# A third buffer for raw weights in a two-layer hybrid encoder step, each unit one transfer with one signal

## The reference, cut to what matters

```
h  = rmsnorm(x, norm_mix)
z  = h @ w_in                     # one projection, 8208 columns: q, k, v | qg, kg, vg, rg | ag | ga, gb
oa = diff_attention(rope(q), rope(k), v, lam)      # 8 heads, two softmax maps a head, cached keys and values
og = gated_linear_attention(qg, kg, vg, decay(ag)) # 4 heads, in chunks of 64 tokens
ua = (rmsnorm(oa) * (1 - lam_init)) @ w_pa
ub = (rmsnorm(og) * silu(rg)) @ w_pb
x += (sigmoid(ga) * ua + sigmoid(gb) * ub) @ w_o
h  = rmsnorm(x, norm_ffn);  x += (silu(h @ w_f1) * (h @ w_f3)) @ w_f2      # inner width 2816
h  = rmsnorm(x, norm_ple);  x += sigmoid(h @ w_ple_gate) * (pe @ w_ple)
```

## Time and profile before

| | |
|---|---|
| time, median of 3 runs | 1424.36 us (1424.17 to 1426.08) |
| the profiled execution | 1431.38 us, its span 1429.6 us |
| PE busy | 1369.6 us, 96% of the span |
| DVE, ACT, POOL busy | 896.6, 620.7, 279.9 us |
| granted TensorE clock, mean | 0.983 of full speed |
| SP's transfers | 180.58 MB; 53.9% of 16 engines' span |
| the chain that ended last | PE 75%, DMA 12%, DVE 9% |

### The profile page before, as it was taken

How to read it: one execution, slowest core, us unless ns; L and a number is a source line. 1 busy time by engine, 2 the same in 40 slices (tenths; PEclk the granted TensorE clock), 3 DMA queues, 4 the chain that set the end, 5 groups by cost and what they waited for, 6 DMA issues and landing times.

```text
span 1429.6 us, 24105 instructions
## 1 busy us (share of the span) xinstructions
PE 1369.6 (96%) x9750; PEld 1326.4 (93%) x9750; DVE 896.6 (63%) x1455; ACT 620.7 (43%) x1043; POOL 279.9 (20%) x321
## 2 busy tenths in 40 slices
PE   6999989999999999999999999888999999999996
PEld 4999988899999999999989899888999999999995
DVE  3868647487666555555777585556775655555454
ACT  3454533546634333333445445334484343333332
POOL 1505031050023000022550231203200500001232
PEclk9999999999999999999999999999999999999998
DMA  7756598664444544444566559975534444454441
GB/s 165 133 119 139 106 107 112 130 139 135 145 139 150 156 147 148 154 146 161 125 117 110 121 134 113 117 99 117 133 125 161 140 151 153 148 157 134 152 150 44
DMA packets 194154, 190.62 MB, mean 133 GB/s; under 512 B 9046, under 2 KB 191132, under 8 KB 194044
## 3 DMA queue, kind: packets, MB, share of 16 engines
q1 hardware_dynamic: 188848, 180.58, 53.9%
q0 software_dynamic: 2688, 7.35, 1.4%
q10 hardware_dynamic: 2508, 1.16, 0.3%
HBM read 180.40 MB, written 8.65 MB: 132 GB/s over the span
## 4 chain that ended last, share of the span: by engine, by line
PE 75%; DMA 12%; DVE 9%; ACT 1%; issue 1%; POOL 0%; SPq 0%; DVEq 0%; POOLq 0%; ACTq 0%
PE big L1255 22%; PE big L1257 21%; PE big L1256 21%; DMA w_raw<-in_w_in 12%; DVE w_lo L849 3%; PE X L1541 1%; PE X L1434 1%; DVE ssq L1005 1%; DVE a_msk L996 1%; PE X L1297 1%; PE X L1466 1%; ACT w_hi L552 1%; PE X L1284 0%; DMA lrow<-in_lambda_k 0%; PE X L1384 0%
## 5 line engine op out<-in xcount | busy, mean ns | idle before, releaser
L1255 PE MATMUL big<-x_hi,w_hi 128*128 128x320 f32 x1856 | 590.7, 318 | 15.1 <-DVE z L939 12.8
L1256 PE MATMUL big<-x_lo,w_hi 128*128 128x320 f32 x1856 | 579.4, 312 | 0.0
L1257 PE MATMUL big<-x_hi,w_lo 128*128 128x320 f32 x1856 | 578.9, 312 | 0.0
L849 DVE TENSOR_TENSOR w_lo<-w_raw,w_hi 128x1024 fp32r<-128x1024 f32 (+1 forms) x328 | 418.6, 1279 | 165.4 <-ACT w_hi L552 163.4
L552 ACT CAST w_hi<-w_raw 128x1024 fp32r<-128x1024 f32 (+1 forms) x328 | 330.4, 1035 | 237.1 <-DMA w_raw<-in_w_in 135.3
L1255 PEld LDWEIGHTS big<-x_hi,w_hi 128*128 128x128 f32 x1856 | 354.1, 191 | 21.2 <-DVE z L939 14.3
L1256 PEld LDWEIGHTS big<-x_lo,w_hi 128*128 128x128 f32 x1856 | 354.1, 191 | 1.3
L1257 PEld LDWEIGHTS big<-x_hi,w_lo 128*128 128x128 f32 x1856 | 353.9, 191 | 0.0
L478 POOL TENSOR_TENSOR sqt<-xT 128x320 f32<-128x320 f32 x48 | 48.0, 999 | 604.8 <-DVE xT L1206 422.5
L1255 PE MATMUL big<-h_hi,w_hi 128*128 128x320 f32 x352 | 108.8, 309 | 0.0
L1257 PE MATMUL big<-h_hi,w_lo 128*128 128x320 f32 x352 | 108.6, 308 | 0.0
(11 more groups left out here) (250 smaller groups left out, 1932.0 us busy)
## 6 DMA issues: line engine op xcount, KB each, us to landing
w_raw<-in_w_in SPq DMA_DIRECT2D x128, 512.0 KB, 8.5
w_raw<-in_w_f SPq DMA_DIRECT2D x120, 512.0 KB, 4.4
w_raw<-in_w_pa SPq DMA_DIRECT2D x16, 512.0 KB, 4.5
w_raw<-in_w_pb SPq DMA_DIRECT2D x16, 512.0 KB, 3.9
w_raw<-in_w_o SPq DMA_DIRECT2D x16, 512.0 KB, 4.0
w_raw<-in_w_ple_gate SPq DMA_DIRECT2D x16, 512.0 KB, 4.7
w_raw<-in_w_f SPq DMA_DIRECT2D x16, 384.0 KB, 3.5
k_raw<-in_cache_k SPq DMA_DIRECT2D x8, 256.0 KB, 10.4
```

Source lines behind the costliest of these rows:

```text
L849: tt(w_lo[:, t % 4, 0:nk, :], w_raw[:, (t // 2) % 2, 0:nk, (t % 2) * P:(t % 2 + 1) * P], w_hi[:, t % 4, 0:nk, :].bitcast(F32), ALU.subtrac ...
L1255: mm(out, wh, xh[:, k0 + k, :], start=start and k == 0, stop=False)
L1256: mm(out, wh, xl[:, k0 + k, :], start=False, stop=False)
L1257: last = mm(out, wl, xh[:, k0 + k, :], start=False, stop=stop and k == nk - 1)
```

## The change

`w_raw` gets a third unit buffer. Where the slot of unit n was that of unit n - 2, it is that of unit n - 3, and SP waits for the splits of unit n - 3 instead of n - 2. A unit is issued as one transfer of 1 MB on one semaphore. Unit 0 of an iteration is still two transfers (qg and kg columns), now with a semaphore each: the `hi` of its first tile waits for the qg half alone (`qg_in`), that of its second tile for the buffer's own semaphore. To make room, `o_sq` no longer has a buffer but lies in the second part of `kcT`. The waits on raw weights are counted from the unit's number.

```diff
+RAW = 3
-    w_raw = sb("w_raw", [P, 2, KC, UW])
+    w_raw = sb("w_raw", [P, RAW, KC, UW])
-        o_sq = sb("o_sq", [P, T], where=where)
+    o_sq = kcT[:, :, :].rearrange("p a b -> p (a b)")[:, 2 * PAST - T:]
-    raw_in = [sem("raw_in0"), sem("raw_in1")]
+    raw_in = [sem(f"raw_in{i}") for i in range(RAW)]
+    qg_in = sem("qg_in")

+        def slot_free(tb, c):
+
+            n = tb // 2 + c
+            if n >= RAW:
+                sp.wait_ge(lo_ready, 2 * (n - RAW + 1) + CREDIT_TILE)
+            return n % RAW
+
         def unit(tb, c, src, row0, nrow, col0):
 
-            sp.wait_ge(lo_ready, tb + (2 * c + CREDIT_TILE - 2))
-            for r in range(0, nrow, nrow // 2):
-                sp.dma_start(w_raw[:, c % 2, r:r + nrow // 2, :],
-                             src[:, bass.ds(row0 + r, nrow // 2), bass.ds(col0, UW)]).then_inc(raw_in[c % 2], 16)
+            i = slot_free(tb, c)
+            sp.dma_start(w_raw[:, i, 0:nrow, :], src[:, bass.ds(row0, nrow), bass.ds(col0, UW)]).then_inc(raw_in[i], 16)
 
         def qk_unit(tb, l, j):
 
-            sp.wait_ge(lo_ready, tb + (CREDIT_TILE - 2))
+            i = slot_free(tb, 0)
             for half, col in enumerate((C_QG, C_KG)):
-                sp.dma_start(w_raw[:, 0, :, half * P:(half + 1) * P],
-                             w_in[:, bass.ds(l * KC, KC), bass.ds(j * P + col, P)]).then_inc(raw_in[0], 16)
+                sp.dma_start(w_raw[:, i, :, half * P:(half + 1) * P],
+                             w_in[:, bass.ds(l * KC, KC), bass.ds(j * P + col, P)]).then_inc(raw_in[i] if half else qg_in, 16)
...
-        def hi(tb, tb8, t, nk):
-
-            act.wait_ge(raw_in[(t // 2) % 2], tb8 + 32 * (t // 4 + 1))
+        def hi(tb, t, nk):
+
+            n = (tb + t) // 2
+            l, m = divmod(tb + t, TILES)
+            if m < MRG_0 and m % MIX_N == 0:
+                act.wait_ge(qg_in, 16 * (l * MIX_IT + m // MIX_N + 1))
+            else:
+                act.wait_ge(raw_in[n % RAW], 16 * (n // RAW + 1))
             act.wait_ge(tile_done, tb + (t + 1))
-            nc.scalar.copy(w_hi[:, t % 4, 0:nk, :], w_raw[:, (t // 2) % 2, 0:nk, (t % 2) * P:(t % 2 + 1) * P]).then_inc(hi_ready, 1)
+            nc.scalar.copy(w_hi[:, t % 4, 0:nk, :], w_raw[:, n % RAW, 0:nk, (t % 2) * P:(t % 2 + 1) * P]).then_inc(hi_ready, 1)
```

More of the change, by code:

```diff
@@ L547, in _ @@
     def _(act):
-        def hi(tb, tb8, t, nk):
-            act.wait_ge(raw_in[(t // 2) % 2], tb8 + 32 * (t // 4 + 1))
+        def hi(tb, t, nk):
[5 more added lines that the diff above has]
+                act.wait_ge(raw_in[n % RAW], 16 * (n // RAW + 1))
             act.wait_ge(tile_done, tb + (t + 1))
-            nc.scalar.copy(w_hi[:, t % 4, 0:nk, :], w_raw[:, (t // 2) % 2, 0:nk, (t % 2) * P:(t % 2 + 1) * P]).then_inc(hi_ready, 1)
+            nc.scalar.copy(w_hi[:, t % 4, 0:nk, :], w_raw[:, n % RAW, 0:nk, (t % 2) * P:(t % 2 + 1) * P]).then_inc(hi_ready, 1)
         def base(l, j, per, first):
-            return act.snap(l * TILES + j * per + first), act.snap(l * (8 * TILES) + j * (8 * per) + 8 * first)
+            return l * TILES + j * per + first
         def tables(which):
@@ L611, in _ @@
             if l == 0:
-                first, first8 = base(l, 0, MIX_N, 0)
-                hi(first, first8, 0, KC)
+                first = base(l, 0, MIX_N, 0)
+                hi(first, 0, KC)
             for m in range(KC if l == 0 else 0):
@@ L617, in _ @@
             if l == 0:
-                hi(first, first8, 1, KC)
+                hi(first, 1, KC)
             else:
@@ L639, in _ @@
             for j in range(0, MIX_IT):
-                tb, tb8 = base(l, j, MIX_N, 0)
+                tb = base(l, j, MIX_N, 0)
                 v = act.snap(l * MIX_IT + j + 1)
@@ L679, in _ @@
                 for t in range(MIX_N):
-                    hi(tb, tb8, t + 2, KC)
+                    hi(tb, t + 2, KC)
                     if j == 0 and t == 1:
@@ L728, in _ @@
                         if j == MIX_IT - 1:
-                            hi(tb, tb8, t + 3, KC)
+                            hi(tb, t + 3, KC)
                         for e in range(2):
@@ L768, in _ @@
             for j in range(OUT_IT):
-                tb, tb8 = base(l, j, OUT_N, OUT_0)
+                tb = base(l, j, OUT_N, OUT_0)
                 for t in range(OUT_N):
-                    hi(tb, tb8, t + 2, KC)
+                    hi(tb, t + 2, KC)
                     if m := j * OUT_N + t:
@@ L779, in up @@
             def up(j, first):
-                tb, tb8 = base(l, j, FUP_N, FUP_0)
+                tb = base(l, j, FUP_N, FUP_0)
                 for t in range(FUP_N):
-                    hi(tb, tb8, t + 2, KC)
+                    hi(tb, t + 2, KC)
                     if first and t == 0:
@@ L799, in _ @@
             for j in range(FDN_IT):
-                tb, tb8 = base(l, j, FDN_N, FDN_0)
+                tb = base(l, j, FDN_N, FDN_0)
                 for t in range(FDN_N):
-                    hi(tb, tb8, t + 2, FDN_K[(t + 2) // 2 % 3])
+                    hi(tb, t + 2, FDN_K[(t + 2) // 2 % 3])
                     m = j * 4 + t // 6 * 2 + t % 2
@@ L812, in _ @@
             for j in range(PLE_IT):
-                tb, tb8 = base(l, j, PLE_N, PLE_0)
+                tb = base(l, j, PLE_N, PLE_0)
                 for t in range(PLE_N):
                     if j < PLE_IT - 1 or t < 2 or l < DEPTH - 1:
-                        hi(tb, tb8, t + 2, KC)
+                        hi(tb, t + 2, KC)
                     if j == t == 0:
```

8 lines of the change are left out of this document (4 added, 4 removed).

## The result

The median fell from 1424.69 us (4 runs, 1424.17 to 1426.08) to **1384.16 us** (4 runs, 1382.18 to 1387.19): a ratio of 0.9727, 95% interval 0.971 to 0.9744, so 38.9 us less by the ratio and 40.5 by the medians. The prediction said 1387.8. The profiled execution took 1384.12 us (span 1382.3, mean granted clock 0.995). It equals its kernel's median, while the profiled execution before, 1431.38 us, was 7.0 above its own. The two profiles therefore lie 47.3 us apart, 7 more than the kernels do.

A forecast was written before the change was run, and what follows sets the result against it. Late weights in the slow `w_in` columns of iteration 3 held up two of eight mixing iterations; 47.6 us less 11.0 staying gives 36.6 off 1431.38, 1394.8, less 7.0 to the median: 1387.8 us, range 1375 to 1402 (8 in 10).

The forecast's parts named there:

- Unit 1 at 874.1: Layer 2's mixing iteration 3: unit 1 lands at 874.1 instead of 880.6, putting the queue 6.5 us further ahead.
- The queue is never empty, today or after, so each landing moves by this much and no more: Third mixing iterations: after unit 1, every landing advances only 6.5 us in layer 2 and 8.6 in layer 1.
- the 5.3 us of lateness at unit 5: Layer 2's mixing iteration 3: unit 5, 11.8 us late before, stays 5.3 us late after the 6.5 us advance.
- the term of 11.0 us that was to stay: Third mixing iterations: 6.9 us of remaining waits (5.3 and 1.6) times 1.59 for slow clock, not gained.
- a factor of 1.59: Third mixing iterations: waiting brings slow clock, 8.9 us on 15.1 idle in layer 2, so waits count 1.59 times.
- The price of unit 7: Mixing iteration 3: unit 7 lands 13.5 us after issue with little ahead of it; the queue is slower than PE there.
- 3.3 us and 1.0 of start: Layer 2's iteration 3: queue starves between unit 6's landing and unit 7's issue; the third buffer removes that gap.
- the slow columns get slower: Third mixing iterations: each slow unit lands 1 us later behind its predecessor; 33.2 us stay, 14.4 go, 1410; chance 0.17.
- The ceiling of 47.6: Mixing stage: summed excess over 75.64 us, plus layer 2's first iteration over layer 1's; at most 47.6 us can go.
- the term of 24.0: Layer 2's mixing iteration 3: 99.65 us less 75.64, so 24.0 us to gain, 15.1 idle and 8.9 slow clock.
- The qg half's own signal: End of layer 2's mixing iteration 3: `attT` wait of 4.21 us goes; removes most of 5.7 us in layer 2's first.
- waits at places not in rows 2: Sign of being wrong: PE waits in the changed kernel at places absent from the earlier profile's listed idle times.

The follow-up runs named there:

- Experiment 4: Changed kernel, but mixing iteration 3 loads the `w_in` columns of iteration 4: 1382.01 us, ratio 0.9705 to the kernel before.
- Experiment 8: Changed kernel, but only unit 7 of a mixing iteration uses the third buffer, other units issued as with two: 1401.23 us, ratio 0.9835 to the kernel before.
- experiment 9: Changed kernel, but unit 7 of a mixing iteration is issued as with two buffers, all others keep the third: 1409.56 us, ratio 0.9894 to the kernel before.
- experiment 5: Kernel before (two buffers), but mixing iteration 3 loads the `w_in` columns of iteration 4: 1400.75 us, ratio 0.9842 to the kernel before.
- Experiment 3: Changed kernel with two buffers and unit 0 awaited whole, leaving one transfer for each other unit: 1422.21 us, ratio 0.999 to the kernel before.
- experiment 2: Changed kernel with two buffers instead of three, keeping merged transfers and the qg half's own signal: 1418.46 us, ratio 0.9969 to the kernel before.
- experiment 1: Changed kernel's three buffers, but two transfers a unit on one semaphore and unit 0 awaited whole: 1386.18 us, ratio 0.9734 to the kernel before.
- Experiment 10: Changed kernel with the loads of `v_past` and `s_past` issued behind unit 5 instead of ahead: 1381.55 us, ratio 0.9699 to the kernel before.
- experiment 6: Changed kernel, but all four mixing iterations load the slow columns of iteration 3: 1412.14 us, ratio 0.9916 to the kernel before.
- experiment 7: Changed kernel unedited, run again for a second profile: 1384.53 us, ratio 0.9723 to the kernel before.

## Why the prediction came out right, by its own steps

- **What bounds the kernel: right.** Two of eight iterations were held up by weights, and the releasers named were a step late. Experiment 4 shows the columns as the reason.
- **Unit 1 at 874.1: right in the number, by luck.** Relative to the start its advance is 6.5 us (layer 2, predicted 6.5) and 9.4 (layer 1, predicted 8.6). Its two terms were both wrong. Unit 0 was to land 10.3 us after its second half was issued, and took 16.8 in layer 2 and 14.0 in layer 1. Unit 1 was to land 12.6 us behind unit 0, and landed 6.1 behind in both. So already unit 1, queued behind another, cost half of the price that I had read where it was issued late.
- **"The queue is never empty, today or after, so each landing moves by this much and no more": wrong, and the step that was mis-sized.** It holds for units 1 to 4. Behind them landings come 5 to 8 us apart (in layer 1 from unit 6 on), and unit 5 of layer 2 lands 17.2 us behind unit 3 instead of 22.8. So the 5.3 us of lateness at unit 5 did not arise, and the term of 11.0 us that was to stay measured 1.7 us in layer 2 (1.2 of it waiting, for unit 4) and 2.0 in layer 1 (1.8 of it a stall that isn't for weights). Beside the floor of experiment 4 it is 2.2 us in the medians, about what such medians can tell at all. The slow clock that I priced with a factor of 1.59 did not come at all: 1.00 in both iterations. So layer 2's iteration took 77.37 us where I had forecast 84, and its one wait was for unit 4, not for unit 5.
- **The price of unit 7 was misread.** I took its 13.5 us as what a slow unit takes. Experiment 8 has the same bytes 8.1 and 9.5 us behind unit 6 when they are queued with it; experiment 9 has 14.1 and 14.4 from issue to landing when they are issued late. It is the price of both. Queued, the slow columns cost twice what fast columns do (8.1 and 9.5 against 3.5 to 4.8 in experiment 8); issued late, fast columns too take 9.1 to 14.0 (experiment 5). The gap of "3.3 us and 1.0 of start" that I let go with the third buffer was in truth 17.1 - 7.8 = 9.3 us in layer 2. By the same lines the rival "the slow columns get slower" went the wrong way.
- **The ceiling of 47.6: too large for the kernel, and short of one stage.** In medians what can go is 1424.69 - 1382.01 = 42.7 us (40.8 beside its own group's 1422.78); 47.6 was read off an execution 7 us above its median, and I took that excess off the time but not off the gain. Experiment 3's profile says where most of it lay, in layer 2's third iteration: by its 93.16 us the term of 24.0 would be 17.5. And I took 77.77 us as what a first iteration needs, where layer 1's now takes 75.53: those 2.2 us were in no term. The final number came out by two errors that cancelled in part, which is luck: 47.6 - 42.7 = 4.9 us too much to gain, 11.0 - 2.2 = 8.8 too much to stay, and 36.6 + 8.8 - 4.9 = 40.5 went.
- **The qg half's own signal: half right.** It is worth 3.75 us with two buffers (experiments 2 and 3), all of it and more in layer 2's first iteration, the place that I had named: from the first matmul of one iteration to that of the next it is 91.55 us there without it and 85.74 with it. With three buffers it is worth nothing that can be told (experiment 1), since the buffer alone takes that wait away. The merged transfer at 0: right (0.999). `o_sq` in `kcT`: no wait turned up; experiments 1 to 3 all had this edit, so it wasn't measured by itself.
- **Where the gain came from.** I put it down to slow columns. Experiment 5 splits it: 1424.13 - 1400.75 = 23.4 us go when only the columns do, and 18.7 more between the kernels without slow columns. The changed kernel removes both, except 2.2. The split isn't one by stages: in the profiles only 10.9 of the 47.3 us lie outside the third iterations.
- **"Landings more than 13 us apart" and "a third iteration above 88 us"** were what would have shown me wrong; the largest distance of units 1 to 7 in the two was 12.6. The third sign, waits at places not in rows 2, did turn up: the stall of 1.8 us at 223.34 is such a place. It is 1.8 us of 1384, and its cause is open. The DMA share of 0.95 in layer 2 was not reached over the iteration (0.91); from unit 1's landing to unit 7's it is 0.95.

The Trainium skill, DMA: Bandwidth & Descriptors (section Anatomy of one DMA — SWDGE (gpsimd) path), gives 4.4 us for 1 MB by its fit, an estimate; the fit is of transfers that GpSimd issues, and SP issues these. The feed-forward rows here (5.1) are near it, the `w_in` rows (10.8 in the median) are not.

**Open.** Why units 5 to 7 of the slow columns come closer behind each other in a backlog than units 2 to 4 do in the same backlog; unit 6 does in every kernel here (7.1 us in the kernel before too), unit 5 in some iterations only (6.4, 11.4). Experiment 10 moved the two cache loads that stand in the queue between units 4 and 5, and did not settle it. The columns of unit 6 may be faster than those of units 2 to 4; no run gave them another place in the queue.

Whether a late unit 7 is slow because its queue was empty or because unit 0 shares the engines with it was not tested, but the profiles say something for fast columns. In the changed kernel's two iterations 2, unit 7 finds the queue empty too, with no unit issued for 15 us behind it, and takes 8.1 and 8.3 us. In the kernel before and in experiment 5, where unit 0 goes out 4 us behind it, it takes 10.1 to 14.0 in the same iterations. So an empty queue is not what makes it slow there, and the company goes with 2 to 6 us more; in the slow columns the two stay together.

The stall of 1.8 us was seen in two of three profiles of the changed kernel and, with 1.5 us, in that of experiment 6. In each of the three, 16 KB of the program's instructions are being loaded 0.4 to 0.7 us ahead of it:

```profile
q1 hardware_dynamic: 93, 0.09, 80.9%
q8 instruction: 1, 0.02, 10.0%
```

(the changed kernel, 221.0 to 221.6 us; the stall begins at 221.55). In the profiles of experiments 1, 7 and 10 this load starts some 4 us earlier against the iteration's start, and there is no stall. Most such loads pass without one (there are 78 in the profile of the changed kernel), and the profile doesn't say whose instructions they are. So a late load of instructions is a candidate that no run tested.

## What to carry to other kernels

Judge a buffer more in a transfer queue by how late the last buffer comes free at its worst place, not by how slow the transfers are: here one unit of eight, issued 15 us behind its neighbour, held half of what the buffer gained. Price a queued transfer by the distance between landings in a backlog; its time from issue to landing, read where it was issued late, was 1.5 to 1.8 times that for unit 7 here. Check each term of a sum by itself even where the sum came out: unit 1 landed where it was forecast by two terms that were each wrong by 6.5 us in layer 2. And hold a profiled execution against its kernel's median before reading a gain off it: time that only this execution lost can't be won.

## What the runs showed of the hardware

- 1 MB of `w_in`'s slow columns lands 5.4 to 12.6 us behind its predecessor in a queue that never empties (table above). Over the same units the engines' time for each MB fell from 8.7 to 7.7 us with the third buffer (two windows above).
- One iteration's columns of `w_in` fill the engines (share 0.91) where another's take 0.62 at the same shapes and strides (experiment 4). I had expected a difference, and not that it is as large: 70.4 us of engine time for 11.0 MB against 0.62 x 75.64 = 46.9 for 134 x 75.64 = 10.1 MB, that is 6.4 against 4.6 us for each MB.
- Unit 7, queued 0.4 us behind unit 6, lands 3.5 to 4.8 us behind it in fast columns and 8.1 and 9.5 in the slow columns (experiment 8).
- One transfer of 1 MB and two of 512 KB made no difference in 1422 us (0.9978 to 1.0002).
